# The sixteen experts of a routed feed-forward layer: the up product in whole rows of 512, and the down product one expert later

## The reference

```python
def expert_choice_ffn(h, w_router, w_gate, w_up, w_down):
    """Each of N_EXPERTS SwiGLU experts picks its top-C tokens of this routed set, C = 2 n / E."""
    n, d = h.shape[1], h.shape[2]
    cap = EC_FACTOR * n // N_EXPERTS
    aff = jax.nn.softmax(jnp.einsum('bnd,de->bne', h, w_router).astype(jnp.float32), axis=-1)
    g, idx = lax.top_k(jnp.swapaxes(aff, 1, 2), cap)
    xin = jax.vmap(lambda hb, ib: hb[ib])(h, idx)
    hid = jax.nn.silu(jnp.einsum('becd,edf->becf', xin, w_gate)) * jnp.einsum('becd,edf->becf', xin, w_up)
    y = jnp.einsum('becf,efd->becd', hid, w_down) * g[..., None].astype(h.dtype)
    return jax.vmap(lambda yb, ib: jnp.zeros((n, d), h.dtype).at[ib.reshape(-1)].add(yb.reshape(-1, d)))(y, idx)
```

## Time and profile before

| | |
|---|---|
| median of 3 runs | 1428.8 us (1427.6 to 1429.22) |
| the profiled execution, whole | 1431.26 us |
| its span, first to last instruction | 1429.5 us |
| expert stage within the span | about 830 to 1390 us |
| PE busy in the span | 1298.7 us (91%) |
| DVE busy | 998.4 us (70%) |
| ACT busy | 765.7 us (54%) |
| DMA | 310.88 MB, mean 217 GB/s |

### The profile page before, as it was taken

How to read it: one execution, slowest core, us unless ns; L and a number is a source line. 1 busy time by engine, 2 the same in 40 slices (tenths; PEclk the granted TensorE clock), 3 DMA queues, 4 the chain that set the end, 5 groups by cost and what they waited for, 6 DMA issues and landing times.

```text
span 1429.5 us, 21032 instructions
## 1 busy us (share of the span) xinstructions
PE 1298.7 (91%) x8073; PEld 1163.8 (81%) x8073; DVE 998.4 (70%) x1315; ACT 765.7 (54%) x868; POOL 85.1 (6%) x108
## 2 busy tenths in 40 slices
PE   6899999799999999998999179999999999999991
PEld 5887899698987999877887068888888888888880
DVE  5858310499556672475544878888888888888886
ACT  6634310233312553572323247777877888777772
POOL 1100000000000000013000000000000000000020
PEclk9999989899999999998999579999999999999995
DMA  9831040000354412304113759999999999999973
GB/s 378 260 88 59 30 148 1 1 1 30 148 206 147 148 60 89 133 1 163 75 74 135 305 211 362 387 389 387 389 391 386 387 391 389 389 386 385 388 268 132
DMA packets 59324, 310.88 MB, mean 217 GB/s; under 512 B 5137, under 2 KB 13361, under 8 KB 29505
## 3 DMA queue, kind: packets, MB, share of 16 engines
q1 hardware_dynamic: 52064, 281.74, 50.6%
q0 software_dynamic: 7200, 28.31, 7.5%
HBM read 282.76 MB, written 35.67 MB: 223 GB/s over the span
## 4 chain that ended last, share of the span: by engine, by line
PE 73%; DVE 14%; ACT 5%; DMA 4%; issue 2%; SPq 0%; POOLq 0%; POOL 0%; DVEq 0%; ACTq 0%
PE psum L2342 23%; PE psum L2002 6%; PE psum L2286 6%; PE psum L2335 4%; PE psum L2333 4%; PE psum L2334 4%; PE psum L2060 4%; PE psum L2062 4%; PE psum L2061 4%; DMA raw<-w_in_units 1%; PE psum L2349 1%; DMA ada_raw<-w_ada_units 1%; DVE ml_c L1458 1%; DVE ml_w L1441 1%; PE psum L1903 1%
## 5 line engine op out<-in xcount | busy, mean ns | idle before, releaser
L1803 DVE TENSOR_TENSOR e_lo<-e_raw,e_hi 128x2048 fp32r<-128x2048 f32 x192 | 435.0, 2288 | 42.0 <-ACT e_hi L1162 40.4
L1162 ACT ACTIVATE e_hi<-e_raw 128x2048 fp32r<-128x2048 f32 x192 | 362.3, 1913 | 53.4 <-PE psum L2342 53.1
L2060 PE MATMUL psum<-w_hi,h_hi 128*128 128x256 f32 x512 | 147.7, 288 | 0.5 <-issue 0.5
L2333 PE MATMUL psum<-e_hi,xt_hi 128*128 128x256 f32 x512 | 147.5, 288 | 0.0
L2062 PE MATMUL psum<-w_lo,h_hi 128*128 128x256 f32 x512 | 146.4, 286 | 0.0
L2061 PE MATMUL psum<-w_hi,h_lo 128*128 128x256 f32 x512 | 146.3, 286 | 0.0
L2335 PE MATMUL psum<-e_lo,xt_hi 128*128 128x256 f32 x512 | 144.9, 283 | 0.0
L2334 PE MATMUL psum<-e_hi,xt_lo 128*128 128x256 f32 x512 | 144.9, 283 | 0.0
L2060 PEld LDWEIGHTS psum<-w_hi,h_hi 128*128 128x128 f32 x512 | 99.9, 195 | 0.7 <-issue 0.6
L2061 PEld LDWEIGHTS psum<-w_hi,h_lo 128*128 128x128 f32 x512 | 99.8, 195 | 0.1
L2062 PEld LDWEIGHTS psum<-w_lo,h_hi 128*128 128x128 f32 x512 | 99.7, 195 | 0.0
(11 more groups left out here) (403 smaller groups left out, 2641.2 us busy)
## 6 DMA issues: line engine op xcount, KB each, us to landing
e_raw<-w_e_units SPq DMA_DIRECT2D x192, 1024.0 KB, 6.9
ada_x<-w_ada_units SPq DMA_DIRECT2D x16, 1024.0 KB, 4.9
raw<-w_in_units SPq DMA_DIRECT2D x14, 1024.0 KB, 6.7
ada_raw<-w_ada_units SPq DMA_DIRECT2D x8, 1024.0 KB, 21.9
xs<-x SPq DMA_DIRECT2D x4, 1024.0 KB, 11.1
acc_dram<-zero_r SPq DMA_DIRECT2D x1, 4096.0 KB, 18.1
wo_raw<-w_out SPq DMA_DIRECT2D x4, 1024.0 KB, 6.0
x_res<-xp_dram SPq DMA_DIRECT2D x4, 1024.0 KB, 7.8
```

Source lines behind the costliest of these rows:

```text
L1162: act.activation(e_hi[u % EH][:], e_raw[u][:], ACT.Copy).then_inc(e_hi_ok, 1)
L1803: dve.tensor_tensor(e_lo[u][:], e_raw[u][:], e_hi[u % EH][:], ALU.subtract).then_inc(e_lo_ok, 1)
L2060: pe.matmul(tok_ps(p, r), x_hi[:, k, c], hi(k), start=k == 0, stop=False)
L2333: pe.matmul(o, x_hi[:, k, :], hi[:, c], start=k == 0, stop=False)
```

## The change

The up matrix is stored and multiplied like the other two: 12 matmuls of 512 columns for a unit, into two whole banks. The hidden layer is then finished all at once, so the order is changed: PE does gate e, up e, and then the down product of expert e-1; in the middle of that stand the eight transposes of the tokens of e+1 and, together, the eight transposes of `hid` of e. The product `hid`, `hd_hi` and `hd_lo` become two steps of 512 columns in place of four of 256. The units are laid out in the order in which they are used; twelve of them are still one turn of the buffers (now called a lap: up e, down e-1, gate e+1). The scatter is issued three experts late in POOL's order. Expert 0 and 1 stand ahead of the loop, with a second pair of token buffers (`xt_hi_1`, `xt_lo_1`). The last expert keeps the four narrow quarters and its down product right behind them (`e_cols`).

```diff
-            def expert_src(e, u):
-                return I["w_e_units"][ds(e, 1), u, :, :].rearrange("o p n -> (o p) n")
-
-            def load_expert_unit(e, u):
-                sp.dma_start(e_raw[u][:], expert_src(e, u)).then_inc(e_full[u], 16)
+            def load_expert_unit(lap, u):
+                sp.dma_start(e_raw[u][:], I["w_e_units"][ds(EU * lap + u, 1), :, :].rearrange("o p n -> (o p) n")).then_inc(e_full[u], 16)
...
-                pool.wait_ge(tok_s_ok, e + 1)
+                pool.wait_ge(tok_s_ok, e + SCATTER_LAG)
...
+            pool.nop().then_inc(tok_s_ok, SCATTER_LAG - 1)
+            for e in (1, 2):
                 pool.wait_ge(xt_mm, e)
                 gather(e)
-                scatter(e - 1)
+            with pool.Fori(SCATTER_LAG, N_EXP) as e:
+                pool.wait_ge(xt_mm, e)
+                gather(e)
+                scatter(e - SCATTER_LAG)
+            scatter(LAST - 2)
+            scatter(LAST - 1)
...
-            def expert_act(e, last):
-                act.wait_ge(w_used, EU * e + 4 + EH)
-                act.activation(hid[:], e_ps(0), ACT.Silu).then_inc(sg_ok, 1)
-                e_split_his(e, (7, 8))
-                hd_hi_part(e, 0)
+                    e_split_hi(lap, u)
+
+            def expert_act(e, first):
+                if not first:
+                    y_out(e - 2, EU * e - 4 + EH, 4)
+                e_split_hi(e - 1, 11)
+                e_split_his(e, range(2))
+                if first:
+                    for b in range(2):
+                        hd_hi_half(0, b, None)
+                e_split_his(e, range(2, 4))
+                gate_silu(e, EU * e + EH, 0)
+                e_split_his(e, range(4, 9))
+                xt_hi_part(e + 1, 2, xt_hi)
                 e_split_hi(e, 9)
-                hd_hi_part(e, 1)
+                hd_hi_half(e, 0, EU * e + 6 + EH)
                 e_split_hi(e, 10)
...
+                hd_hi_half(e, 1, EU * e + 8 + EH)
...
+            e_split_his(0, range(EH, 8))
+            gate_silu(0, 4 + EH, 0)
+            e_split_his(0, range(8, 10))
+            xt_hi_part(1, 4, xt_hi_1)
+            e_split_hi(0, 10)
+            expert_act(1, True)
+            with act.Fori(2, LAST) as e:
                 expert_act(e, False)
-            expert_act(N_EXP - 1, True)
+            y_out(LAST - 2, EU * LAST - 4 + EH, 4)
+            e_split_hi(LAST - 1, 11)
+            e_split_his(LAST, range(3))
+            y_out(LAST - 1, EU * LAST + EH, 0)
+            e_split_his(LAST, range(3, 7))
...
+            def hid_half(e, b, used):
+                if b == 0:
+                    dve.wait_ge(sg_ok, e + 1)
+                    dve.wait_ge(w_used, used)
+                h = hid[:, BANK * b:BANK * (b + 1)]
+                dve.tensor_tensor(h, h, e_ps(2)[:, BANK * b:BANK * (b + 1)], ALU.mult).then_inc(hid_ok, 2)
...
-            def expert_dve(e, last):
-                hid_part(e, 0)
-                e_split_lo(e, 7)
-                hid_part(e, 1)
-                e_split_lo(e, 8)
-                hd_lo_part(e, 0)
-                hid_part(e, 2)
-                e_split_lo(e, 9)
-                hd_lo_part(e, 1)
-                hid_part(e, 3)
-                e_split_lo(e, 10)
-                hd_lo_part(e, 2)
-                if not last:
-                    xt_lo_part(e + 1)
-                hd_lo_part(e, 3)
-                e_split_lo(e, 11)
-                if not last:
-                    e_split_los(e + 1, range(7))
+                    e_split_lo(lap, u)
+
+            def expert_dve(e, first):
+                e_split_lo(e - 1, 11)
+                e_split_los(e, range(2))
+                if first:
+                    for b in range(2):
+                        hd_lo_half(0, b)
+                e_split_los(e, range(2, 7))
+                hid_half(e, 0, EU * e + 4 + EH)
+                hid_half(e, 1, EU * e + 4 + EH)
+                e_split_los(e, range(7, 9))
+                xt_lo_part(e + 1, 2, xt_hi, xt_lo)
+                hd_lo_half(e, 0)
+                e_split_los(e, range(9, 11))
+                hd_lo_half(e, 1)
...
+            def e_rows(lap, u, i, x_hi, x_lo, o):
...
-                if 4 <= u < 8:
-                    for k in range(KC):
-                        c = slice(UW * k, UW * (k + 1))
-                        pe.matmul(o, x_hi[:, k, :], hi[:, c], start=k == 0, stop=False)
-                        pe.matmul(o, x_lo[:, k, :], hi[:, c], start=False, stop=False)
-                        i = pe.matmul(o, x_hi[:, k, :], lo[:, c], start=False, stop=k == KC - 1)
-                else:
-                    for j in range(2):
-                        k = 2 * (u % 4) + j
-                        for x, w in ((x_hi, hi), (x_hi, lo), (x_lo, hi)):
-                            a, z = k == 0 and x is x_hi and w is hi, k == KC - 1 and x is x_lo
-                            for b in range(2):
-                                i = pe.matmul(o[:, BANK * b:BANK * (b + 1)], x[:, k, :], w[:, D * j + BANK * b:D * j + BANK * (b + 1)],
-                                              start=a, stop=z)
-                i.then_inc(w_used, 1)
-
-            def x_transposes(e):
+                for j in range(2):
+                    k = 2 * i + j
+                    for x, w in ((x_hi, hi), (x_hi, lo), (x_lo, hi)):
+                        a, z = k == 0 and x is x_hi and w is hi, k == KC - 1 and x is x_lo
+                        for b in range(2):
+                            m = pe.matmul(o[:, BANK * b:BANK * (b + 1)], x[:, k, :], w[:, D * j + BANK * b:D * j + BANK * (b + 1)],
+                                          start=a, stop=z)
+                m.then_inc(w_used, 1)
...
-            def expert_pe(e, last):
+            def expert_pe(e, first, x_hi, x_lo):
                 pe.wait_ge(xt_ok, e + 1)
-                for u in range(4):
-                    e_unit(e, u, xt_hi, xt_lo, e_ps(0))
-                for q in range(4):
-                    e_unit(e, 4 + q, xt_hi, xt_lo, quarter(2, q))
-                    if q:
-                        hid_transposes(e, q - 1)
-                if not last:
-                    x_transposes(e + 1)
-                hid_transposes(e, 3)
-                pe.wait_ge(y_free, e + 1)
-                for u in range(8, EU):
-                    pe.wait_ge(hd_ok, 4 * e + u - 8 + 1)
-                    e_unit(e, u, hd_hi, hd_lo, e_ps(4))
+                for i in range(4):
+                    lap, u = (e - 1, 8 + i)
+                    e_rows(lap, u, i, x_hi, x_lo, e_ps(0))
+                    if first and i == 1:
+                        hid_transposes(0)
+                for i in range(4):
+                    e_rows(e, i, i, x_hi, x_lo, e_ps(2))
+                pe.wait_ge(y_free, e)
+                for i in range(4):
+                    pe.wait_ge(hd_ok, 4 * e - 4 + i + 1)
+                    e_rows(e, 4 + i, i, hd_hi, hd_lo, e_ps(4))
+                    if i == 1:
+                        pe.wait_ge(hid_ok, 4 * e + 4)
+                        x_transposes(e + 1, 2)
+                        pe.wait_ge(hd_ok, 4 * e)
+                        hid_transposes(e)
 
             pe.wait_ge(route_ready, 1)
-            x_transposes(0)
-            with pe.Fori(0, N_EXP - 1) as e:
-                expert_pe(e, False)
-            expert_pe(N_EXP - 1, True)
+            x_transposes(0, 6)
+            pe.wait_ge(xt_ok, 1)
+            for i in range(4):
+                e_rows(0, i, i, xt_hi, xt_lo, e_ps(0))
+            for i in range(4):
+                e_rows(0, 4 + i, i, xt_hi, xt_lo, e_ps(2))
+                if i == 1:
+                    x_transposes(1, 4)
+            expert_pe(1, True, xt_hi_1, xt_lo_1)
+            with pe.Fori(2, LAST) as e:
+                expert_pe(e, False, xt_hi, xt_lo)
+            for i in range(4):
+                pe.wait_ge(hd_ok, 4 * LAST - 4 + i + 1)
+                e_rows(LAST - 1, 8 + i, i, hd_hi, hd_lo, e_ps(0))
...
-    rows = lambda w: w.reshape(N_EXP, 4, 2, P, D).transpose(0, 1, 3, 2, 4).reshape(N_EXP, 4, P, 2 * D)
-    cols = up.reshape(N_EXP, KC, P, 4, UW).transpose(0, 3, 2, 1, 4).reshape(N_EXP, 4, P, 2 * D)
-    return np.ascontiguousarray(np.concatenate([rows(gate), cols, rows(down)], 1))
+    rows = lambda w: w.reshape(4, 2, P, D).transpose(0, 2, 1, 3).reshape(4, P, 2 * D)
+    cols = lambda w: w.reshape(KC, P, 4, UW).transpose(2, 1, 0, 3).reshape(4, P, 2 * D)
+    parts = [rows(gate[0]), rows(up[0])]
+    for e in range(1, N_EXP - 1):
+        parts += [rows(gate[e]), rows(up[e]), rows(down[e - 1])]
+    z = N_EXP - 1
+    parts += [rows(down[z - 1]), rows(gate[z]), cols(up[z]), rows(down[z])]
```

More of the change, by code:

```diff
@@ L103 @@
 EH = 4
+SCATTER_LAG = 3
 def build(nc, I, out):
@@ L135, in build @@
         ident = small("ident", [P, P])
+        GATE_ROWS_AT = off[0]
         gate_rows = small("gate_rows", [P, ALL])
@@ L1165, in xt_hi_part @@
                 act.wait_ge(xt_mm, e + 1)
[L1166 to L1180 removed]
```

(79 more changed lines are left out.)

88 lines of the change are left out of this document (42 added, 46 removed).

## The result

The changed kernel takes 1419.31 us (median of 5 runs, 1417.07 to 1420.19), the kernel before in the same comparison 1429.22 (1427.6 to 1434.13). The ratio is 0.9934 with a 95% interval of [0.9919, 0.9948]: 9.9 us less (7 to 12 by the interval), where 10.0 were predicted; the median was forecast at 1418.8. The profiled span went from 1429.5 to 1417.5 us.

A forecast was written before the change was run, and what follows sets the result against it. PE was taken to bound the expert stage. Savings of 8.7 (wide up product) and 1.8 (gather), less 0.4 (prologue) and 0.1 (last expert), gave 10.0 us: 1428.8 to 1418.8 us; forecast 1417.5 to 1420.5, 8-in-10 range 1416.8 to 1424.

The forecast's parts named there:

- The bound: Expert stage: PE, busy without a gap, sets the pace; ACT and DVE follow and loads arrive in time; period 35.17 us.
- The wide up product: Up product, experts 0 to 14: 96 matmuls at 0.1196 us become 48 at 0.2271, 0.58 us each, 8.7 us saved.
- The gather: Token transposes: the gather issued ahead of the scatter removes PE's 0.14 us wait per expert, 1.8 us saved.
- The wait for `hid`: Middle of the down product: PE's new wait costs nothing, some 2.3 us spare; rival of a slower kernel, chance 0.05.
- The prologue: End of expert 0's up product: ACT and DVE squeeze leaves PE idle 0.4 us, from 0 to 1.
- The last expert: Two `y_exp` behind adjacent down products: 0.1 us lost; a scatter slower by 2 us would cost 0.9.
- The loads: Expert stage: 34.8 us of DMA needed per expert against a 34.45 us period; 15 us of cover, so no cost.
- the queue falls behind by 0.35 us per expert: DMA queue in the expert stage: need over the new period adds up to 4.5 us in 13 experts, absorbed by cover.
- the sign that I named: Load landing times should grow along the expert stage from about 8 us at most to 11 or 12.
- The DMA rival: Expert stage: loads become the bound, giving back 4.9 us, 1423.7 us, with ACT waiting for loads; chance 0.10.
- The chances: Whole kernel: forecast range 0.72; faster by more than 0.2% 0.91, within 0.2% 0.04, slower 0.05.
- the seams: Prologue, first loop turn and adjacent down products cost more, plus one similar hold-up: 1420.5 to 1423 us; chance 0.10.

The follow-up runs named there:

- the repeated comparison: The changed kernel unaltered, run again beside other kernels on another chip, against the kernel before: 1420.18 us, ratio 0.9933 [0.9912, 0.9954].

## Why the prediction was right, step by step

That the two medians of the main comparison differ by 9.9 us, 0.1 from the forecast, is luck: the repeated comparison gave 8.8, and the interval is about 4 us wide. What the runs bear out are the terms.

- **The bound.** PE's pace set the stage, as read from the waits and the chain. Right: 9.0 us came from PE's instructions alone, with the order held.
- **The wide up product**, 8.7 us: 8.3 to 9.0 between the stages with and without it, and 9.0 between the medians. The distance of 0.2271 us held in the new place, 0.2268.

  The traces have 111.4, 119.6 and 226.9 ns at 128, 256 and 512 columns. The rule of the Trainium skill (TensorE: Matmul & The Clock Gate, Back-to-back issue gap: N / 2.4 + 2.5 ns), by which 1.8 us of the gain were left, an estimate, has 55.8, 109 and 216 and doesn't agree. The same section says that the rule is for a matmul by itself, and that in a stream with weight loads it is too low at small N and too high at large N, with about 81 ns at 128 and 131 at 512. At 128 the direction agrees with the run (111.4 is above 55.8) and the size doesn't; at 512 neither does (226.9 is above 216).
- **The gather**, 1.8 us: 1.9 in the stage of the kernel that has it alone. Right in size, though between runs of whole kernels it is within the uncertainty.
- **The wait for `hid`**, nothing: right, 2.7 us spare. The experiments show that this was the step to worry about. One split too many ahead of it costs 5 to 6 us of the gain, two turn it into a loss of 36. The order in which DVE takes its splits around `hid` carries the change as much as the width does.
- **The prologue**, 0.4 us of idle: right in place, some 0.25 us in size. The chain goes through `xt_lo` as worked out:

```profile
855.79 1.14 DVE xt_lo L1846
...
856.98 5.83 PE psum L2400 x24
```

  PE's last three starts stand at 855.83, 856.28 and 856.98 in its timeline, where 0.45 is the usual step of two matmuls.
- **The last expert**, 0.1: PE shows no idle time there.
- **The loads.** The conclusion held (nobody waits for one), a term was mis-sized. I took 5.0 us for gather and scatter out of one stretch of 27.3 us; it is 3.7. The need is 33.5 us per expert, not 34.8, and it was below the period before the change and after it. So the step "the queue falls behind by 0.35 us per expert" is wrong, and with it the sign that I named: landing times were to grow to 11 or 12 us. They didn't. For loads issued from 900 to 950 us, and from 1290 to 1340, where they should have been longest (from 1290 to 1340 the kernel before had 4.6/7.1/8.2):

```profile
DMA to landing us min/median/max: 7.6/9.0/9.8
...
DMA to landing us min/median/max: 4.9/6.9/8.3
```

- **The DMA rival** (chance 0.10) is thereby answered. It would need a period under 33.5 us. The next 0.9 us that PE loses per expert would still be a gain, and what lies beyond would not.
- **The chances.** The 0.91 for "faster" is added up wrongly: the forecast, the seams and the DMA case alone are 0.92.

Why did gather and scatter seem to take 5.0 us in the stretch of the kernel before? The sum took the queue to be busy to its full rate all along. But that stretch moved 391 GB/s, and a full queue 407 to 421. By the later prices, 9 x 2.48 + 3.7 = 26.0 us, some 1.3 us of the 27.3 were slack. How the slack comes about stays open, and so does why landing times in the changed kernel stay between 5 and 10 us, although the need is 0.9 us per expert below the period.

## What to carry to other kernels

Where PE is busy without a gap, read its cost as the distance between matmuls at each width, and multiply by the count: a column count doubled saved 12 ns per pair here, and 9 us in 1420. But a wider product is finished later as a whole, so look for what was overlapped by pieces; put independent work (the next up product) between it and its consumer, and count the engine queue in front of the consumer to within one instruction. To find how near a second bound is, take work off the first one and read the new period, and do not add up one stretch of the old trace, nor trust a busy share of 1.01: compare the GB/s of the stretch with those of a full queue.

## What the runs showed of the hardware that I had not expected

- A matmul of 128 columns costs 111.4 ns (one run), one of 256 costs 119.6: halving the columns from 256 saves next to nothing.
- A block of eight transposes behind a wait of PE takes 1.09 us in the chain, without a wait 0.87, after a wait of 0.2 us as after one of 2.9. In the period such a wait costs some 0.2 us more than the idle time that the profile shows: 0.38 for 0.17, and 3.11 for 2.89. The timelines show where most of it lies. Idle time is counted from the modelled end of the last wide matmul, 0.39 us after its start, while the next would have started 0.23 after it. From the block's first start to the one behind it are 0.93 us, not 0.87. In the kernel before, where the tokens came only a little late, the block took 0.91 us.
- The single core moved 421 GB/s over 100 us with its engines busy. The prediction set 358 GB/s from the Trainium skill (DMA: Bandwidth & Descriptors, Specifications) against 423 in the trace. Another page of the Trainium skill (HBM Reference, Specifications (TRN2)) takes 358 for the share when both cores of a pair stream, and gives about 425 GB/s for a core that streams alone; with that the trace agrees. The prediction's estimate of 35.1 us from the first of the two counted the twelve loads alone, without gather and scatter.
- A scatter of 128 rows that adds in DRAM takes 9.4 to 10.0 us to land beside the loads in the kernel before and 9.2 to 11.8 in the changed one, but only 2.4 us of the queue's capacity; latency and capacity differ by a factor of four.
